# VectorE instead of GpSimd sums the FFNs' token quadrants; weight sums of the second pair and one lo half moved

## What is computed

```python
# first block
x = x + ga1 * rmsnorm(mixer(h) @ w_o, post_mix_g)
h = rmsnorm(x, pre_ffn_g) * (1.0 + sc2) + sh2
gate, up = split(h @ w_ffn_in)
x = x + ga2 * rmsnorm((silu(gate) * up) @ w_ffn_out, post_ffn_g)
# second block
x = x + concat(fox_out, diff_out) @ w_out
h = rms_norm(x, ffn_norm_g)
x = x + (silu(h @ w_gate) * (h @ w_up)) @ w_down
```

## Time and profile before

| what | value |
|---|---|
| median of 3 runs | 1431.53 us (1431.49 to 1432.14) |
| profiled execution, its own time | 1431.97 us |
| its span in the profile | 1430.2 us |
| PE busy | 1373.4 us, 96% of the span |
| DVE busy | 992.4 us, 69% |
| ACT busy | 707.7 us, 49% |
| POOL busy | 152.6 us, 11% |
| mean granted clock of TensorE | 0.987 of full speed |

### The profile page before, as it was taken

How to read it: one execution, slowest core, us unless ns; L and a number is a source line. 1 busy time by engine, 2 the same in 40 slices (tenths; PEclk the granted TensorE clock), 3 DMA queues, 4 the chain that set the end, 5 groups by cost and what they waited for, 6 DMA issues and landing times.

```text
span 1430.2 us, 19665 instructions
## 1 busy us (share of the span) xinstructions
PE 1373.4 (96%) x7800; PEld 1184.5 (83%) x7800; DVE 992.4 (69%) x1371; ACT 707.7 (49%) x1145; POOL 152.6 (11%) x111
## 2 busy tenths in 40 slices
PE   8999999999899999999999999999679999999996
PEld 6888888787579999988876888887567999998885
DVE  5798997695787878884237545667777778877332
ACT  4466886633465555662235334454345565655221
POOL 2197335000030000000002000000003000000000
PEclk9999999999999999999999999999889999999998
DMA  9423112467302323316321322110120323232321
GB/s 365 157 78 99 45 44 89 149 212 284 106 16 89 115 93 118 134 61 220 102 89 44 104 75 73 45 45 15 43 105 15 119 89 118 89 133 89 103 88 59
DMA packets 41131, 147.28 MB, mean 103 GB/s; under 512 B 4560, under 2 KB 4816, under 8 KB 40912
## 3 DMA queue, kind: packets, MB, share of 16 engines
q1 hardware_dynamic: 40896, 143.93, 30.0%
q10 hardware_dynamic: 144, 2.10, 0.3%
HBM read 143.91 MB, written 2.10 MB: 102 GB/s over the span
## 4 chain that ended last, share of the span: by engine, by line
PE 84%; DVE 8%; ACT 4%; issue 2%; DMA 1%; DVEq 0%; SPq 0%; ACTq 0%
PE ps L1467 27%; PE ps L1468 26%; PE ps L1469 26%; PE ps L1590 1%; DMA raw<-in_wo 1%; PE ps L1827 1%; ACT w_hi L455 1%; DVE t_buf L956 1%; DVE w_lo L908 1%; DVE t_buf L942 1%; PE ps L1506 1%; PE ps L1814 1%; DVE x L951 1%; PE ps L1535 0%; PE ps L1501 0%
## 5 line engine op out<-in xcount | busy, mean ns | idle before, releaser
L1467 PE MATMUL ps<-h_hi,w_hi 128*128 128x256 f32 (+1 forms) x1160 | 391.3, 337 | 9.9 <-DVE w_lo L908 6.8
L1469 PE MATMUL ps<-h_hi,w_lo 128*128 128x256 f32 (+1 forms) x1160 | 387.6, 334 | 0.0
L1468 PE MATMUL ps<-h_lo,w_hi 128*128 128x256 f32 (+1 forms) x1160 | 387.5, 334 | 0.0
L908 DVE TENSOR_TENSOR w_lo<-raw,w_hi 128x1024 fp32r<-128x1024 f32 x141 | 189.9, 1349 | 120.1 <-ACT w_hi L455 119.5
L1467 PEld LDWEIGHTS ps<-h_hi,w_hi 128*128 128x128 f32 x1160 | 220.7, 190 | 38.4 <-DVE w_lo L908 9.3
L1469 PEld LDWEIGHTS ps<-h_hi,w_lo 128*128 128x128 f32 x1160 | 220.6, 190 | 22.1
L1468 PEld LDWEIGHTS ps<-h_lo,w_hi 128*128 128x128 f32 x1160 | 220.9, 190 | 20.8 <-issue 0.5
L455 ACT ACTIVATE w_hi<-raw 128x1024 fp32r<-128x1024 f32 x141 | 148.3, 1054 | 152.3 <-PE ps L1469 82.9
L898 DVE TENSOR_TENSOR w_lo<-quads,w_hi 128x1024 fp32r<-128x1024 f32 (+1 forms) x152 | 164.9, 1086 | 76.4 <-ACT w_hi L455 76.4
L455 ACT ACTIVATE w_hi<-quads 128x1024 fp32r<-128x1024 f32 (+1 forms) x152 | 144.3, 949 | 78.0 <-PE ps L1469 78.0
L1467 PE MATMUL ps<-act_hi,w_hi 128*128 128x512 f32 x352 | 137.0, 389 | 0.0
(11 more groups left out here) (266 smaller groups left out, 2205.9 us busy)
## 6 DMA issues: line engine op xcount, KB each, us to landing
quads<-in_ffn_in SPq DMA_DIRECT2D x76, 512.0 KB, 4.4
raw<-in_ffn_out SPq DMA_DIRECT2D x44, 512.0 KB, 3.8
raw<-in_ada SPq DMA_DIRECT2D x32, 512.0 KB, 4.3
raw<-in_qk SPq DMA_DIRECT2D x25, 512.0 KB, 3.7
ada<-in_ada SPq DMA_DIRECT2D x16, 512.0 KB, 9.1
raw<-in_gates SPq DMA_DIRECT2D x16, 512.0 KB, 3.7
raw<-in_v SPq DMA_DIRECT2D x12, 512.0 KB, 3.6
raw<-in_ffn_in SPq DMA_DIRECT2D x12, 512.0 KB, 3.7
```

The lines of the kernel that those rows point to most:

```text
L908: nc.vector.tensor_tensor(w_lo[p % RING][:], raw[q % RAW][:], w_hi[p % RING][:].bitcast(f32), ALU.subtract).then_inc(raw_used, 1)
L1467: nc.tensor.matmul(out, w[0], v[0], start=start, stop=False, **kw)
L1468: nc.tensor.matmul(out, w[0], v[1], start=False, stop=False, **kw)
L1469: return nc.tensor.matmul(out, w[1], v[0], start=False, stop=stop, **kw)
```

## The change

Three edits. The four token sums of each FFN go from POOL to DVE: s1 and s2 behind the lo half of panel 2, then the lo half of panel 3, then s4 and s3. The weight sums of pair 1 go from the projection ahead of the FFN into turn 0 of the seven-product loop. In `wout_step` the `feed` of every even m but 0 goes behind the addition to x. What each computes stays the same.

```diff
--- before.py
+++ after.py
@@ -405,18 +405,6 @@
                     pool.wait_ge(pool_tap, n - 1)
                 nc.gpsimd.tensor_tensor(conv[:, c, :], conv[:, c, :], tap_buf[n % 3][:], ALU.add).then_inc(pool_tap, 1)
 
-            def by_seven(s):
-                a11, a12 = h_f[:, 0:HALF, 0:TOK], h_f[:, HALF:KT, 0:TOK]
-                a21, a22 = h_f[:, 0:HALF, TOK:SEQ], h_f[:, HALF:KT, TOK:SEQ]
-                pool.wait_ge(hf_ready, KT * (s + 1))
-                nc.gpsimd.tensor_tensor(s_f["s1"][:], a21, a22, ALU.add).then_inc(s_made, 1)
-                pool.wait_ge(s_made, 4 * s + 1)
-                nc.gpsimd.tensor_tensor(s_f["s2"][:], s_f["s1"][:], a11, ALU.subtract).then_inc(s_made, 1)
-                pool.wait_ge(s_made, 4 * s + 2)
-                nc.gpsimd.tensor_tensor(s_f["s4"][:], a12, s_f["s2"][:], ALU.subtract).then_inc(s_made, 1)
-                nc.gpsimd.tensor_tensor(s_f["s3"][:], a11, a21, ALU.subtract).then_inc(s_made, 1)
-
-            by_seven(0)
             pool.wait_ge(h_ready, 3 * KT)
             nc.gpsimd.memset(sel_f[:], 0.0).then_inc(consts2, 1)
             nc.gpsimd.memset(pos_i[:], 0).then_inc(consts2, 1)
@@ -426,7 +414,6 @@
                 nc.gpsimd.affine_select(out=sel_f[:], in_=sel_f[:], compare_op=ALU.not_equal, fill=-1.0, base=-off,
                                         pattern=[[-1, HEADS], [0, P]], channel_multiplier=1).then_inc(consts2, 1)
                 pool.wait_ge(consts2, 4 + n)
-            by_seven(1)
 
         @block.scalar
         def _(act):
@@ -1126,9 +1113,9 @@
             for m in range(KT):
                 feed("wo", m, dots=m < 3)
                 add_square(KT + m)
-                if m in (4, 5):
-                    first_sums(0, m - 4)
-                    second_sums(0, m - 4)
+                if m == 4:
+                    first_sums(0, 0)
+                    second_sums(0, 0)
             dve.wait_ge(raw_used, AT[FIRST["ffn_in1"]])
             link(nc.vector.tensor_tensor(mod[:, 16:40], mod[:, 16:40], col("ada_b", 16, 24), ALU.add))
             link(nc.vector.tensor_tensor(gain[:, 1, :], mod[:, 16:24], col("post_mix_g", 0, KT), ALU.mult))
@@ -1156,8 +1143,28 @@
                     nc.vector.tensor_tensor(s_lo[which][:], s_f[which][:], s_hi[which][:].bitcast(f32),
                                             ALU.subtract).then_inc(s_lo_of, 1)
 
+                def first_token_sums():
+
+                    a11 = h_f[:, 0:HALF, 0:TOK]
+                    a21, a22 = h_f[:, 0:HALF, TOK:SEQ], h_f[:, HALF:KT, TOK:SEQ]
+                    dve.wait_ge(hf_ready, KT * (s + 1))
+                    nc.vector.tensor_tensor(s_f["s1"][:], a21, a22, ALU.add).then_inc(s_made, 1)
+                    dve.wait_ge(s_made, 4 * s + 1)
+                    nc.vector.tensor_tensor(s_f["s2"][:], s_f["s1"][:], a11, ALU.subtract).then_inc(s_made, 1)
+
+                def second_token_sums():
+                    a11, a12 = h_f[:, 0:HALF, 0:TOK], h_f[:, HALF:KT, 0:TOK]
+                    a21 = h_f[:, 0:HALF, TOK:SEQ]
+                    dve.wait_ge(s_made, 4 * s + 2)
+                    nc.vector.tensor_tensor(s_f["s4"][:], a12, s_f["s2"][:], ALU.subtract).then_inc(s_made, 1)
+                    nc.vector.tensor_tensor(s_f["s3"][:], a11, a21, ALU.subtract).then_inc(s_made, 1)
+
                 for i in range(PLAIN):
                     feed(name, 2 * i)
+                    if i == 0:
+                        first_token_sums()
+                        feed(name, 1)
+                        second_token_sums()
                     if i == 1:
                         sum_lo(2)
                     feed(name, 2 * i + 1)
@@ -1188,7 +1195,7 @@
                 for j in range(BY_SEVEN):
                     n, (bank_a, bank_b, bank_c) = pairs0 + j, banks_of(j)
                     last = j == BY_SEVEN - 1
-                    more = 0 < j < BY_SEVEN - 1
+                    more = j < BY_SEVEN - 1
                     feed(seven, UNIT_N[j, 0])
                     if j:
                         second_tokens(j - 1)
@@ -1434,18 +1441,20 @@
             dve.wait_ge(x_add["wout_a"], KT)
 
             def wout_step(m):
-                if m % 2 == 0:
-                    feed("wout_b", m // 2)
+                if m == 0:
+                    feed("wout_b", 0)
                 dve.wait_ge(*half_last("wout_b", m))
                 nc.vector.tensor_tensor(x[:, m, :], x[:, m, :], ps[:, WOUT_BANK[m], :], ALU.add)\
                     .then_inc(x_add["wout_b"], 1)
+                if m and m % 2 == 0:
+                    feed("wout_b", m // 2)
             wout_step(0)
             for m in range(1, KT):
                 wout_step(m)
                 add_square(5 * KT + m - 1)
-                if m in (3, 4):
-                    first_sums(1, m - 3)
-                    second_sums(1, m - 3)
+                if m == 3:
+                    first_sums(1, 0)
+                    second_sums(1, 0)
             add_square(6 * KT - 1)
             normalise(3, 6, lambda k: col("ffn_norm_g_2", k), kept=1)
             ffn_in(1)
```

## The result

The changed kernel took 1423.65 us (median of 4, 1422.98 to 1427.8) against 1431.67 us before (median of 4). The ratio is 0.9939, with a 95% interval from 0.9923 to 0.9954. The forecast was 1424.5, in a range of 1422.7 to 1427.8.

What follows compares the result with a forecast made beforehand. PE, busy for 96% of a 1430.2 us span, was taken as the bound, so only its holes count. Gains of 1.65 + 1.61 + 2.53 + 1.20 = 7.0 us against 1431.53 gave 1424.5 us, range 1422.7 to 1427.8.

Steps and rivals of the forecast that it cites:

- Token sums: Before plain tiles 2 and 4 of both FFNs: moving four sums to DVE gains 1.65 and 1.61 us.
- the chain of product, hi halves and lo halves: First FFN, up to panel 4: DVE's first plain product, 1.1 us late, delays what follows; 0.5 us of hole stays.
- the second hole: PE's idle before plain tile 4; in the second FFN it was to go wholly, 0.76 us with its extra cost.
- That POOL's work caused the slow rows: DVE beside POOL in the FFNs: sharing costs DVE 6.3 us, against 4.8 us for four sums on DVE itself.
- The Trainium skill's warning: Shifting work between GpSimd and VectorE might not help; by it only 3.7 us gained, 1427.8 us, chance 0.08.
- The rival that sums are slow on DVE: In both FFNs each sum takes 2.98 us on DVE instead of 1.21: 7.2 us slower, 1438.7 us, chance 0.04.
- Weight sums: Pair 1's sums leave DVE's chain in `wout_b` for turn 0 of the seven-product loop: gain 2.53 us.
- the cover: Seven-product loop, unit (1, 0): its lo half ends 1.3 us before PE needs it, so no loss there.
- The lo half: In `wout_b`, additions moved ahead fill DVE's holes at m = 2 and m = 6, 0.60 us each: gain 1.20.
- The clock: Line 1501's pair behind `wout_b` stays at 2.08 us; rival, clock stays up: 1.04 us more gain, 1423.5, chance 0.15.
- The sum: Whole kernel: the two FFN gains, weight sums and lo half add up to 7.0 us, giving 1424.5 us.

Runs made afterwards that it cites:

- the repetition: The changed kernel timed and traced once more with no edit, against the kernel before: 1426.24 against 1433.32 us, ratio 0.9944.
- the fillers: The changed kernel with 12 extra matmuls on PE in the idle stretch behind `wout_b`, in groups of 6, 4 and 2: ratio 0.9940 to the kernel before.

## Why the prediction was right

- **Token sums: 1.65 and 1.61 forecast, 1.54 and 1.59 in the trace.** No row had shown such a sum on DVE, and the cost per sum, taken from the lo half's row as 1.21, measured 1.22. The missing 0.1 in the first FFN is DVE's queue, 12.84 us in place of 12.73: each of its steps is about 0.01 longer. That what is late next is the chain of product, hi halves and lo halves is shown twice: two more sums move tile 4 by 2.5 us, and taking panel 4's halves out from behind the others closes the last 0.6. In the second FFN the number came out partly for another reason than forecast. The working let PE set tile 4, 28.40 us behind the pair, with DVE ready 0.13 us earlier. In the traces DVE's queue starts 15.54 us behind the pair, as before, and ends 12.84 later, which is 28.4 as well, and it is the later of the two: the repetition waits 0.42 us for it, so the second hole is not gone for good, and panel 4's halves taken first gain 0.60 there.
- **That POOL's work caused the slow rows** was the argument for the edit and is shown: with POOL busy beside it DVE is back at 2.58 for panel 2's lo half, and its sums take 3.3. The Trainium skill's warning (Perfetto Trace Analysis, Optimizing Scalar/DVE Operations) names a read port of SBUF that the two share. The traces agree in that DVE slows down beside POOL; that it is this port no run here singles out. Its "might not help" stands in advice on relieving a full VectorE by giving work away; as a rule against this edit, which is how the prediction weighed it, it does not hold here, where the shift ends the sharing and gains 2.9 us alone.
- **The rival that sums are slow on DVE** did not come true: `h_f` in four runs of 256 is no hindrance. What it would have cost was seen only with POOL at work beside it, where two sums of 3.3 to 3.4 us and a lo half of 3.36 made the kernel slower than before.
- **Weight sums: 2.53 forecast, 2.54 measured**, and nothing lost in the loop. The lo half of unit (1, 0) came at 438.82, 2.53 behind the first sum, and ended 1.3 us before PE used it: the cover as forecast.
- **The lo half: 1.20 forecast and measured**, two steps of an addition.
- **The clock:** the pair stayed at 2.08, as forecast, and a clock that stayed up would have gained 1.0 us, as the fillers showed. This term was nearer to failing than a chance of 0.15 says. In the changed kernel the granted clock is 0.50 in 1060.00 to 1060.40 and the pair starts at 1060.89; in the repetition it is 0.79 in 1062.00 to 1062.40 and the pair starts at 1062.68; with panel 4's halves first it is still 1.00 in 1054.80 to 1055.20, with the pair at 1055.28 and again 2.08 long.
- **The sum: 7.0 forecast, 6.85 in the stages.** The timings say 8.7 and 8.0 us by their ratios (0.9939 and 0.9944), with intervals that hold 6.85, which is a ratio of 0.9952. The remaining 1 to 2 us are not settled, since most timed executions have no trace. Stages outside the change do differ by that much: the first 77 matmuls took from 22.64 to 25.05 us over all fourteen traces, and the 120 matmuls around the hole of 2.08 us ahead of `wout_b` 23.91 to 23.95 us in seven of them, where the granted clock stayed at full, and 25.35 to 25.58 in the other seven, where it was at half for a while. Whether the change makes the shorter form more likely is open.

## What to carry to other kernels

Before work is given to GpSimd because it is idle, look at what VectorE's rows last while GpSimd works: here 11.9 us of GpSimd's work slowed VectorE by about 6.3 us in one FFN, more than the 4.9 (four rows of 1.22) that the same work took on VectorE itself. Where one engine's queue sets the end of a stage, place work that is not due there behind the point where the other engine has a surplus, and put ahead of a wait whatever does not need it. And read such small edits by the length of stages in the traces, from the same matmul to the same matmul: they repeated to 0.1 us where the timings spread over 7.

## What was not expected of the hardware

Executions of one kernel spread over 7 us (1429.41 to 1436.62 in 28), and a part of it lies where PE has short holes: after the same hole of 2.08 us the granted clock is at half in one execution of the changed kernel and at full in another, and the stretch takes 25.35 us or 23.94. Second, while POOL's and DVE's sums ran side by side, both of two float32 inputs, four of POOL's took 12.35 us and DVE's about 3.3 each, so each instruction of DVE lasted a little longer than one of POOL's, 3.1. POOL's four had taken 11.9 in the kernel before, also beside DVE; how long they take alone no run shows.
